# A second gate/up job on plain weight blocks in each FFN, and a reordered DVE and ScalarE list

## The reference

```python
D_MODEL, D_FF = 1024, 2816

def _swiglu(x, w_gu, w_down):
    a, b = jnp.split(x @ w_gu, 2, axis=-1)
    return (jax.nn.silu(a) * b) @ w_down

def _trunk(x, ...):
    for i in range(DEPTH):
        x = x + 0.5 * _swiglu(_rmsnorm(x, norm_g[i, 0]), ffn_gu[i, 0], ffn_down[i, 0])
        hn = _rmsnorm(x, norm_g[i, 1])
        ...                                   # retention or gated DeltaNet
        x = x + m
        x = x + 0.5 * _swiglu(_rmsnorm(x, norm_g[i, 2]), ffn_gu[i, 1], ffn_down[i, 1])
    return _rmsnorm(x, final_g), ...
```

## Time and profile before

| | us |
|---|---|
| median of 3 runs | 2654.21 |
| lowest, highest | 2649.24, 2656.33 |
| the profiled execution | 2644.7 |
| its span | 2643.1 |
| PE matmul busy in the span | 2487.6 (94%) |
| DVE busy | 1832.4 (69%) |
| ACT busy | 1096.0 (41%) |
| POOL busy | 816.9 (31%) |

### The profile page before, as it was taken

How to read it: one execution, slowest core, us unless ns; L and a number is a source line. 1 busy time by engine, 2 the same in 40 slices (tenths; PEclk the granted TensorE clock), 3 DMA queues, 4 the chain that set the end, 5 groups by cost and what they waited for, 6 DMA issues and landing times.

```text
span 2643.1 us, 48562 instructions
## 1 busy us (share of the span) xinstructions
PE 2487.6 (94%) x19567; PEld 2385.8 (90%) x19567; DVE 1832.4 (69%) x2596; ACT 1096.0 (41%) x1810; POOL 816.9 (31%) x643
## 2 busy tenths in 40 slices
PE   6999999999999989999989999999999998899997
PEld 6999999898989889999979999989998998899997
DVE  7777776646464687777787777777557756877774
ACT  5444443424242454444444443444433344434443
POOL 4333322202020243333243333312530453433331
PEclk8999999999999989999999999999999999999999
DMA  3233333424242323333323333321122122233231
GB/s 114 86 91 96 96 106 127 177 96 172 96 171 96 136 72 89 96 97 96 97 72 89 88 96 96 114 86 51 49 69 82 35 61 57 65 96 94 85 103 57
DMA packets 295881, 247.96 MB, mean 94 GB/s; under 512 B 9940, under 2 KB 276364, under 8 KB 295664
## 3 DMA queue, kind: packets, MB, share of 16 engines
q1 hardware_dynamic: 281312, 197.32, 24.8%
q0 software_dynamic: 14352, 47.58, 5.2%
HBM read 218.81 MB, written 26.05 MB: 93 GB/s over the span
## 4 chain that ended last, share of the span: by engine, by line
PE 67%; DVE 24%; ACT 4%; issue 4%; DMA 0%; POOL 0%; DVEq 0%; ACTq 0%; SPq 0%; POOLq 0%
PE ps L1586 24%; PE ps L1218 18%; DVE wl L2193 9%; PE ps L1607 5%; PE ps L1402 4%; PE ps L1025 3%; DVE x L2281 3%; DVE hl L2275 2%; DVE ps L2247 2%; DVE gated L2251 2%; ACT hh L1792 2%; PE ps L1113 1%; PE ps L1136 1%; DVE ps L2237 1%; PE ps L1122 1%
## 5 line engine op out<-in xcount | busy, mean ns | idle before, releaser
L1586 PE MATMUL ps<-xch,wh 128*128 128x260 f32 x2352 | 676.8, 288 | 97.7 <-DVE x L2281 58.5
L1586 PE MATMUL ps<-xch,wl 128*128 128x260 f32 x2352 | 670.6, 285 | 0.0
L1586 PE MATMUL ps<-xcl,wh 128*128 128x260 f32 x2352 | 669.8, 285 | 0.0
L1586 PEld LDWEIGHTS ps<-xch,wh 128*128 128x128 f32 x2352 | 449.3, 191 | 112.4 <-DVE x L2281 69.5
L1586 PEld LDWEIGHTS ps<-xcl,wh 128*128 128x128 f32 x2352 | 448.7, 191 | 0.0
L1586 PEld LDWEIGHTS ps<-xch,wl 128*128 128x128 f32 x2352 | 448.1, 191 | 0.0
L2193 DVE TENSOR_TENSOR wl<-raw,wh 128x1024 fp32r<-128x1024 f32 (+1 forms) x204 | 273.3, 1341 | 21.3 <-ACT wh L1748 21.1
L1218 PE MATMUL ps<-xh,wh 128*128 128x260 f32 x1280 | 269.7, 292 | 1.5 <-DVE rot L2415 0.8
L1218 PE MATMUL ps<-xh,wl 128*128 128x260 f32 x1280 | 260.3, 285 | 0.0
L1218 PE MATMUL ps<-xl,wh 128*128 128x260 f32 x1280 | 260.1, 285 | 0.0
L1778 ACT ACTIVATE kept<-ps 128x260 f32<-128x260 f32 x252 | 96.5, 386 | 331.3 <-PE ps L1586 330.0
(11 more groups left out here) (429 smaller groups left out, 5175.6 us busy)
## 6 DMA issues: line engine op xcount, KB each, us to landing
raw<-in_ffn_gu_dram SPq DMA_DIRECT2D x128, 512.0 KB, 5.1
raw_third<-in_ffn_gu_dram SPq DMA_DIRECT2D x48, 512.0 KB, 4.8
raw<-in_ret_w_in_dram SPq DMA_DIRECT2D x48, 512.0 KB, 4.4
raw<-in_ffn_down_dram SPq DMA_DIRECT2D x80, 256.0 KB, 3.0
s_ring<-in_state_ret_dram POOLq DMA_DIRECT2D x32, 512.0 KB, 6.4
out_dram<-s_ring POOLq DMA_DIRECT2D x32, 512.0 KB, 3.5
raw<-in_gdn_w_in_dram SPq DMA_DIRECT2D x32, 512.0 KB, 5.1
raw_third<-in_ffn_down_dram SPq DMA_DIRECT2D x48, 256.0 KB, 2.9
```

The lines of the kernel that those rows point to most:

```text
L1586: m_ = nc.tensor.matmul(o, w_, r_, start=m in (1, 2, 5) and t == 0 and n == 0, stop=t == KP - 1 and n == 2, skip_group_check=m in (3, 4, 6 ...
```

## The change

- Job 1 is now whole too (`WHOLE = 2`, 96 matmuls instead of 84). Its up half runs first, into banks 2 and 3; its gate half then goes to banks 6 and 7 as soon as `sr.0` has left them. Job 0's up half moves to banks 4 and 5.
- The differences of x are made in pieces (`MIXED_IN`): some in job 0, the rest in job 1's list, with `silu_scaled` and `whole_product` of job 0 in between. In FFN 0 and 3 these are tiles 0, 1 and then 2, 3 (before all four in job 0), in FFN 1 tiles 1, 2 and then 3 (before 1, 2, 3), in FFN 2 tile 3 in job 1 (before in job 0). The reciprocal comes that much earlier in DVE's list.
- In the first FFN the splits of job 0's weights come earlier (`WEIGHTS_AT[0] = (2, 4)`, before 4 and 7), and the input transposes use banks 0 to 3.
- `NORM_AT` places `norm_sum`: in FFN 0 after two tiles of job 1's up half, elsewhere before tile 7 of job 0, as before. ACT loads silu's table right after the square root, by a silu of one column (`table`).
- In a down job that follows a gate job and precedes one, DVE no longer splits group "2" before the x updates; the split comes after them. This holds for the sixteen (D, G) pairs of each FFN.
- Between two gate jobs the split "4" moves into the second one, after `hl` on DVE and after `m1` on ACT, and ACT copies `u2` before it makes `hh`.
- The last down job of FFN 1 uses banks 2 to 5 (before 6, 7, 4, 5), so FFN 2's first gate product doesn't wait for its x update.

```diff
-WHOLE_BLOCKS = {"A": (2, 3), "L": (4, 6)}
+WHOLE = 2
+WHOLE_BLOCKS = ({"A": (2, 3), "L": (6, 7)}, {"L": (0, 1), "A": (4, 5)})
...
-        UP = ps[:, 2:4, 0:HALF]
+        UP = (ps[:, 4:6, 0:HALF], ps[:, 2:4, 0:HALF])
+        WEIGHTS_AT = ((2, 4), (4, 7), None, (4, 7))
-        MIXED_FROM = (0, 1, 3, 0)
-        NORM_AT = ((6,), (7,), (7,), (7,))
+        MIXED_IN = (((0, 1), (2, 3)), ((1, 2), (3,)), ((), (3,)), ((0, 1), (2, 3)))
+        NORM_AT = (1, 0, 0, 0)
...
         def down_banks(f, j, n):
-            if j == NJ - 1 and f < 3:
+            if j == NJ - 1 and f in (0, 2):
...
+                for part in "LA":
+                    if part == "A":
+                        v("sr.0")
...
+                    for n in range(KT):
+                        if part == "L" and n == 2 and NORM_AT[f] == 1:
+                            norm_sum(NORM_IN[f])
+                        whole(1, part, n)
...
# ACT, a gate job
                         if gate_before:
                             silu(p)
+                        if is_whole(p):
+                            block_split(f, j, "L")
                         copy(j, "m1", 1, 0)
                         if gate_before:
-                            h_high(p)
-                        if is_whole(p):
                             block_split(f, j, "4")
                         high("A")
                         copy(j, "u2", 6, 1)
+                        if gate_before:
+                            h_high(p)
                         high("x")
                         copy(j, "m5", 5, 3)
-                        high("12Lyz4")
+                        high("12Lyz")
...
# DVE, a whole job
+                        if j:
+                            whole_scaled(p)
+                        else:
+                            low("L")
+                        todo = MIXED_IN[f][j]
+                        for n, t in enumerate(todo):
                             x_mixed(f, t)
+                            if n:
+                                x_split(f, todo[n - 1])
+                            elif j:
+                                silu_scaled(p)
+                                whole_product(p)
+                        if todo:
+                            x_split(f, todo[-1])
...
# DVE, a gate job
                         if not gate_before:
+                            block_split(f, j, "2")
                             block_split(f, j, "L")
                             block_split(f, j, "4")
...
# DVE, a down job after a gate job
                         first(p)
                         h_low(p)
-                        low("2yz")
+                        low("yz")
```

150 lines of the change are left out of this document (80 added, 70 removed).

## The result

| | before | after |
|---|---|---|
| median of the runs, us | 2651.72 (4 runs) | 2534.18 (4 runs) |
| lowest, highest | 2638.92, 2656.33 | 2531.09, 2538.09 |
| span of the profiled execution | 2643.1 | 2529.5 |

The ratio is 0.9565, with a 95% interval of 0.9528 to 0.9602. A second set of runs of the kernel after, beside the experiments, gave a median of 2540.59 us (2534.40 to 2547.73, 6 runs) against 2647.04 (11 runs): 0.9600, 0.9569 to 0.9632. The forecast of 2543.4 us was 9 us above the first median and 3 us above the second.

What follows compares the result with a forecast made beforehand. PE, busy 94%, was taken to lose time to x-update stalls in the pairs and waits at the FFN starts. Gains 67.2 + 43.6 = 110.8 us, from 2654.21, gave 2543.4 us; 8-in-10 range 2526 to 2590.

Steps and rivals of the forecast that it cites:

- part 1: In the 64 (D, G) pairs, x updates ahead of split "2" remove PE's stall of 1.05 us each: 67 us.
- the split of 1.2 to 1.8 us: Sign to look for in the profile after: split "2" on DVE still takes 1.2 to 1.8 us in its new place.
- 132 matmuls at 0.121 us ... are 15.95 to 16.05 us: PE's time for one pair without the stall, against 17.06 us now; leaves 1.0 to 1.1 us, taken as 1.05.
- The slack of 0.3 us: In the pair, split "2" in its new place ends at 173.65, 0.3 us ahead of product 6's need.
- rival 1: The pair's stall moves from product 2 to product 6, as POOL holds split "2": 2575 us, at worst 2611; chance 0.17.
- Part 2: FFN starts: second whole job and differences in pieces, gaining 10.4, 8.9, 14.1 and 10.2 us, 43.6 together.
- The step to `sr.0`: FFN 0: PE starts at about 19.3, waits some 6 us for `sr.0` at 47.0; FFN 1 and 3: no wait.
- From `sr.0` on there are ... 34.8 us, plus what is left of waits between gate jobs, for which I take 1.5 us in each FFN: From `sr.0` to the first down job: 288 matmuls, 34.8 us, plus 1.5 us of waits; 1 us more in FFN 3.
- rival 2: The FFN starts give half, because DVE lags behind with one more weight split: 2543 + 22 = 2565 us; chance 0.15.
- FFN 2's banks: FFN 2's start: other banks avoid PE's 3.63 us wait for FFN 1's last x update, less 0.8; inside FFN 2's 14.1.
- Part 3: ACT's list between gate jobs: with `hh` behind `u2`, product 7 finds its copy in time; counted inside the starts' 43.6 us.

Runs made afterwards that it cites:

- experiment 1: Kernel after with split "2" moved back ahead of the x updates in the 64 pairs: 2612.2 us, 0.9874 of the kernel before.
- experiment 2: Kernel before with only split "2" moved behind the x updates, nothing else changed: 2565.7 us, 0.9690 of the kernel before.
- experiment 7: Kernel after with two or four unused DVE reductions ahead of split "2" in the 64 pairs: 2546.4 us with two, 2626.1 us with four.
- experiment 5: Kernel after with job 2's split "2" behind `gr.1` on DVE, and ACT's "2" and "L" behind m1: 2532.1 us, beside 2540.6 for the kernel after.
- experiment 3: Kernel after with ACT again making `hh` ahead of splits "4", "A" and copy `u2` between gate jobs: 2541.2 us, 0.9600 of the kernel before.
- experiment 4: Kernel after with all remaining x differences made in each FFN's first job instead of in pieces: 2546.8 us in its second set, 0.9613 of the kernel before.
- experiment 8: Kernel after with FFN 1's last down job back in the kernel before's banks and order: 2537.9 us, 0.9607 of the kernel before.

## Why the prediction was right, and where it wasn't

**What bounds the kernel, and part 1.** Right, and shown by experiments 1 and 2, which undo and make the same move: the stall in the pair hung on split "2" standing ahead of the x updates. It took POOL as well, as the forecast says, and the kernel before has its own experiment on that. In one pair of each FFN POOL's sum came late, since it waited for its weights, and the split got in first (DVE, then POOL):

```profile
272.85 0.68 DVE L2193 TENSOR_TENSOR wl<-raw_third,wh 128x512 fp32r<-128x512 f32 x1
...
273.17 1.52 POOL L797 TENSOR_TENSOR mixed<-raw 128x512 f32<-128x512 f32 x1 [0.80 <-DMA raw<-in_ffn_gu_dram]
```

In these four pairs the split took 0.68 us, and PE lost at most 0.4 us; in the other 60 it took 1.77 to 1.79, and PE stood. The new order came out as forecast: the split of 1.2 to 1.8 us took 1.70, POOL's instruction held it, and PE found it in time. No wait took the place of the one removed.

The size was off. The step that failed is "132 matmuls at 0.121 us ... are 15.95 to 16.05 us": a pair takes 15.80, which is 0.1197 for a matmul. I had divided the shown busy time, tails included, by the count, where the distance between the starts of matmuls was to be read. The trace of the kernel before held what was needed. The matmul ahead of the wait of the earlier trace rows starts at 172.42 and is shown with 0.28 us, a tail of 0.16, and the second one behind the wait starts 0.20 after the first:

```profile
173.88 0.28 PE L1586 MATMUL ps<-xcl,wh 128*128 128x260 f32 x1
```

So the stall cost 0.98 + 0.16 + 0.08 = 1.22 us, not 1.05. By the pair's windows it is 17.06 - 15.80 = 1.26. The count was off too: I took 64 stalls and put the 61 waits of the earlier trace rows down to missing records, but four pairs had none. The middles fell by 74.3 us, which is 60 x 1.24. The term was 67.2, 64 x 1.05.

**The slack of 0.3 us, and rival 1.** The slack was real and it was 0.1 to 0.2. That it held in nearly all pairs is shown by the missing row of waits. Had POOL's instruction been half a microsecond later, rival 1 would have held in part: experiment 7 shows that beyond the slack each pair pays in full.

**Part 2, the second whole job.** The step to `sr.0` was right: PE started at 19.07 (forecast 19.3) and waited 6.62 us in FFN 0 until 46.75 (forecast some 6, until 47.0), and in FFN 1 to 3 the gate half of job 1 found `sr.0` there or all but so (7.0 us of waits in all, 6.6 of them in FFN 0). What failed is the step behind it: "From `sr.0` on there are ... 34.8 us, plus what is left of waits between gate jobs, for which I take 1.5 us in each FFN". The sum was 43.6 and measured 28.1, in two parts:

- In FFN 1 to 3 a wait of 2.79, 2.84 and 3.02 us ahead of product 6 of job 2, with half clock behind it. In FFN 1 the 14 matmuls to 943.21 then cost 14 x 0.10 = 1.4 us more, so 4.4 us with the tail, against a shortfall of 8.9 - 4.8 = 4.1. I had counted DVE's work up to `sr.0` and then only PE's, and hadn't gone on to `gr.1`, the next thing that PE would wait for through silu and m1. Experiment 5 shows that these waits hang on the splits that stand ahead of m1. It gave back 1.2 to 2.2 us of the 3.3 to 4.4 that each of the three FFNs fell short, and other waits came behind it.
- In FFN 0 waits of 1.40, 0.32, 0.85, 0.72 and 0.43 us between gate jobs, 3.7 us and about 4.9 with 0.24 for each, where I had 1.5, and half clock over the 26 matmuls up to 52.33, 26 x 0.095 = 2.5 us, where I had 2:

```profile
42.09:52.33 10.24, 5.58 (x26) 0.50 0.31 84
```

So rival 2 ("the starts give half", because DVE "lags behind") was nearer to the starts' mechanism than the forecast was. Its size, 22 us, was nearer too: 28.1 came, and the forecast had 43.6.

The second whole job was not undone by itself. Of the 28.1 us, PE's earlier start in FFN 0 (19.07 instead of 22.70) is 3.6, and experiments 3, 4 and 8 put 3.3 to 4.2, 3.5 to 4.4 and 0 to 0.6 on ACT's list, the pieces and the banks. That leaves 15 to 18 us for the second whole job by subtraction, if the parts add up; no run shows it.

**FFN 2's banks.** Forecast at about 3.6 less 0.8 inside the 14.1. FFN 2 gave 10.8 net, but experiment 8 shows that the banks themselves account for at most 0.6 of it. With the old banks the wait is 1.46 us instead of 3.63. The pair's order isn't what shortened it (in experiment 2 it is 3.65). The rows under experiment 8 put it down to job 1's sums, which POOL no longer makes and DVE no longer meets. The forecast counted on that for one POOL instruction in FFN 0 and nowhere else.

**Part 3.** Right: experiment 3 puts it at 3.3 to 4.2 us, within the sum of part 2, and product 7 now finds its copy in time at every step. The ten waits for ACT's copies that are left stand ahead of product 6, by the count of matmuls between them, and are for m1: the three long ones, and seven of 0.64 to 1.40 us, which the forecast had only as its 1.5 us of rest for each FFN.

**Why the sum was near all the same.** The pairs gave 7.1 us more and the starts 15.5 less, which is 8.4 short: 102.4 instead of 110.8. The profiled executions differ by 113.6 since the one before had the two stretches at half clock in the retention stage. So it was luck that the forecast of 110.8 came this near: two errors of opposite sign, and a difference in a stage that the change doesn't touch. How many of the runs behind the medians of 2651.7 and 2534.2 had such stretches isn't known. The second set, 2540.6 against 2647.0, gives 106.5.

## What to carry to other kernels

Cost a stall by the distance between the starts of the instructions on both sides of it: with 0.1197 us between matmuls, a shown wait of 1 us cost 1.25. Where an engine's list is shortened, follow the waits past the first one that goes, through every engine in the chain, until something is found that is early; here the next one (`gr.1`, silu, m1) was late in three FFNs, which fell 11.8 us short of a forecast of 43.6. A sum that one engine no longer has to make can also free another that it held, as POOL did DVE here. And when a part of two profiles differs where the code doesn't, take a second profile of the same kernel before explaining it.

## What the runs showed of the hardware that I had not expected

- PE fell to a grant of 0.50, for 10.24 or 3.41 us at a time, in the retention stage while the profile shows it busy without a gap. Two stretches of 10.24 us cost 9.3 us (527.3 against 517.9 for the same kernel); they came in some executions of the same kernel and not in others. Over the 13 profiles without the one of 6160 us there are 22 such falls, all at four places, one for each head of the stage: some 80, 208, 336 and 464 us into it, less what earlier falls had cost. Each began within 0.9 us of the start of the last of sixteen matmuls of one column. (Four more falls, of 3.41 us, stand near the end of the stage; the one in the kernel before came behind a wait of 1.92 us.) This is the row of sixteen ahead of the fall at 621.47 in the kernel before:

```profile
619.24 1.84 PE L1136 MATMUL ps<-ones,sq 128*128 128x1 f32 x16
```

- The four stretches at half clock shown above had a DMA share of 0.75 to 0.79 and 275 to 300 GB/s. In its first profile the kernel after passed three of these places at a grant of 1.00 with 0.75 to 0.87 and 285 to 314 GB/s (467 to 478, 723 to 734, 852 to 863 us), so the DMA traffic by itself doesn't decide it. What does stays open.
- A wait of 2.79 us came with half clock behind it, and one of 2.61 us that ended at 911.64 in the same profile was followed by 3.41 us at 0.50 from 912.49 on; waits of 0.4 to 1.2 us in job 2 of FFN 1 to 3 (experiment 5) had none.
- A DVE reduction beside a POOL instruction took 0.68 us, and so did a split behind it, where the split beside POOL took 1.70. Putting 1.20 us of work ahead of the split delayed its end by 0.18.
- In one execution of 6160 us the matmuls took 2.5 times their time though the clock shown as granted was 1.00, while a DVE instruction took 0.70 us on the mean as usual. This window of it lies among the pairs of FFN 0, and below it is one of the same kind from the kernel after:

```profile
400.00:420.00 20.00, 20.00 (x67) 20.00 (x67) 4.87 (x7) 2.67 (x5) 0.34 (x1) 1.00 0.09 27
```

```profile
200.00:220.00 20.00, 20.00 (x170) 20.00 (x169) 16.33 (x23) 8.04 (x14) 6.85 (x5) 1.00 0.46 130
```

Here 67 matmuls filled 20 us, there 170 did (the columns are PE, PEld, DVE, ACT, POOL, then the granted clock, DMA share and GB/s). The cause stays open.
